# Issuing the scores of two narrow attention steps together, and moving four pieces of work, in a one-core hybrid decoder layer

## The reference, cut to what matters

```python
def dsa_attention(q_lat, kv_lat, q_idx, k_idx, w_idx, bias_tab):   # A: 8 heads
    ...
    logits = jnp.einsum('bqhc,bqkc->bqhk', ql, kv_sel) * ATTN_SCALE + bias
    ...
    p = jax.nn.softmax(logits, axis=-1).astype(kv_sel.dtype)
    return jnp.einsum('bqhk,bqkc->bqhc', p, kv_sel)

def diff_attention(q, k, v, lam, bias_tab):                        # B: 4 heads, 2 maps each
    ...
    logits = jnp.einsum('bqhmd,bshmd->bmhqs', qb, k) * ATTN_SCALE + bias
    logits = jnp.where(dist >= 0, logits.astype(jnp.float32), -jnp.inf)
    p = jax.nn.softmax(logits, axis=-1)
    attn = (p[:, 0] - lam * p[:, 1]).astype(v.dtype)
    return jnp.einsum('bhqs,bshe->bqhe', attn, v)
```

## Time and profile before

| what | value |
|---|---|
| time, median of 3 (lowest to highest) | 1002.81 us (1002.26 to 1003.08) |
| profiled execution: time, span | 1003.18 us, 1001.4 us |
| granted TensorE clock, share of full | 0.998 |
| TensorE busy | 984.4 us, 98% of the span |
| VectorE, ScalarE, GpSimd busy | 481.1 (48%), 378.6 (38%), 102.5 us (10%) |
| branch B and its drain | about 355 to 426 us of the span |

### The profile page before, as it was taken

How to read it: one execution, slowest core, us unless ns; L and a number is a source line. 1 busy time by engine, 2 the same in 40 slices (tenths; PEclk the granted TensorE clock), 3 DMA queues, 4 the chain that set the end, 5 groups by cost and what they waited for, 6 DMA issues and landing times.

```text
span 1001.4 us, 12705 instructions
## 1 busy us (share of the span) xinstructions
PE 984.4 (98%) x4925; PEld 805.3 (80%) x4925; DVE 481.1 (48%) x827; ACT 378.6 (38%) x679; POOL 102.5 (10%) x137
## 2 busy tenths in 40 slices
PE   7999999999999999999999999999999999999997
PEld 5778888878878767788788888988888888888886
DVE  4754777832244445564655563643433333331324
ACT  5345422254466666443223233542322322221222
POOL 1500000000064612200000002000000000000401
PEclk9999999999999999999999999999999999999999
DMA  8884226312131201255555642123344334222312
GB/s 329 261 267 140 85 84 174 99 43 85 63 108 32 64 23 32 74 197 174 182 183 204 221 153 84 63 84 105 108 142 153 120 105 147 84 105 84 126 43 84
DMA packets 88163, 123.13 MB, mean 123 GB/s; under 512 B 4824, under 2 KB 69941, under 8 KB 87986
## 3 DMA queue, kind: packets, MB, share of 16 engines
q1 hardware_dynamic: 87442, 115.98, 35.4%
q0 software_dynamic: 528, 6.22, 2.1%
q10 hardware_dynamic: 144, 0.26, 0.1%
HBM read 119.77 MB, written 8.45 MB: 128 GB/s over the span
## 4 chain that ended last, share of the span: by engine, by line
PE 91%; DMA 3%; DVE 2%; issue 2%; ACT 1%; POOL 1%; SPq 0%; POOLq 0%; DVEq 0%; ACTq 0%
PE tile_ps L859 18%; PE tile_ps L861 18%; PE tile_ps L860 18%; DMA w_raw<-in_w_in_dram 2%; PE t_ps L1125 2%; PE s_ps L1107 2%; PE o_ps L1154 2%; PE tile_ps L1303 1%; PE s_ps L1304 1%; PE s_ps L1303 1%; PE t_ps L1304 1%; PE t_ps L1303 1%; PE tile_ps L1302 1%; PE tile_ps L1304 1%; PE s_ps L1302 1%
## 5 line engine op out<-in xcount | busy, mean ns | idle before, releaser
L859 PE MATMUL tile_ps<-h_hi,w_hi 128*128 128x512 f32 x736 | 291.4, 396 | 1.6 <-DVE w_lo L1814 1.0
L860 PE MATMUL tile_ps<-h_lo,w_hi 128*128 128x512 f32 x736 | 286.9, 390 | 0.0
L861 PE MATMUL tile_ps<-h_hi,w_lo 128*128 128x512 f32 x736 | 286.8, 390 | 0.0
L1814 DVE TENSOR_TENSOR w_lo<-w_raw,w_hi 128x2048 fp32r<-128x2048 f32 (+3 forms) x60 | 131.3, 2189 | 162.1 <-ACT w_hi L1428 162.1
L859 PEld LDWEIGHTS tile_ps<-h_hi,w_hi 128*128 128x128 f32 x736 | 138.1, 188 | 38.9 <-issue 8.2
L861 PEld LDWEIGHTS tile_ps<-h_hi,w_lo 128*128 128x128 f32 x736 | 138.2, 188 | 29.4
L860 PEld LDWEIGHTS tile_ps<-h_lo,w_hi 128*128 128x128 f32 x736 | 138.3, 188 | 27.4 <-issue 0.2
L1428 ACT ACTIVATE w_hi<-w_raw 128x2048 fp32r<-128x2048 f32 (+3 forms) x60 | 107.3, 1788 | 42.7 <-PE tile_ps L861 9.1
L1811 DVE TENSOR_TENSOR t_lo<-t_raw,t_hi 128x2048 fp32r<-128x2048 f32 (+1 forms) x15 | 32.8, 2184 | 85.6 <-ACT t_hi L1426 85.5
L1426 ACT ACTIVATE t_hi<-t_raw 128x2048 fp32r<-128x2048 f32 (+1 forms) x15 | 27.0, 1799 | 81.5 <-PE s_ps L1304 53.5
L1573 ACT ACTIVATE nl<-nl,cst 128x256 f32<-128x256 f32 (+3 forms) x81 | 42.8, 529 | 35.8 <-DVE cst L2023 35.3
(11 more groups left out here) (404 smaller groups left out, 1680.8 us busy)
## 6 DMA issues: line engine op xcount, KB each, us to landing
w_raw<-in_w_in_dram SPq DMA_DIRECT2D x31, 1024.0 KB, 5.4
w_raw<-in_w_gate_up_dram SPq DMA_DIRECT2D x22, 1024.0 KB, 7.0
ada<-in_w_ada_dram SPq DMA_DIRECT2D x12, 1024.0 KB, 5.5
t_raw<-in_w_down_dram SPq DMA_DIRECT2D x10, 1024.0 KB, 5.0
row_copies<-row_flat POOLq DMA_DIRECT2D x1, 5632.0 KB, 21.5
ada<-in_w_ada_dram SPq DMA_DIRECT2D x8, 640.0 KB, 11.5
ada<-in_w_ada_dram SPq DMA_DIRECT2D x8, 512.0 KB, 4.3
ada<-in_w_ada_dram SPq DMA_DIRECT2D x8, 384.0 KB, 10.0
```

Source lines behind the costliest of these rows:

```text
L859: pe.matmul(dst[0:mw, :], wh, x_hi[:, kx, :], start=start, stop=False)
L860: pe.matmul(dst[0:mw, :], wh, x_lo[:, kx, :], start=False, stop=False)
L861: mm = pe.matmul(dst[0:mw, :], wl, x_hi[:, kx, :], start=False, stop=stop)
L1814: dve.tensor_tensor(w_lo[s][:, 0:kt, 0:n_cols], w_raw[s][:, 0:kt, 0:n_cols], w_hi[s][:, 0:kt, 0:n_cols].bitcast(F32), ALU.subtract) \
```

## The change

Scores in branch B: at every step with v % 4 == 0 TensorE now issues the scores of v and of v + 1 together, in the order map 0 of v, map 0 of v + 1, map 1 of v, map 1 of v + 1; those of v + 1 are written to columns 128 to 383 of the same bank. Steps with v % 4 == 1 issue no scores. VectorE's shift waits for the whole bank.

Gate tiles: Z_STEPS changes, so that steps 69, 73 and 77 have no dense piece, and 75, 79 and 83 have one. The high part of chunk 22 follows its tile; its low part stays at step 76.

GpSimd: `power(2, ...)` now stands ahead of `row_copies`, and the copies wait for the high part of chunk 4 (the third of its buffer) and no longer for h.

Branch A's reciprocals: both steps of a pair are done at the odd step.

```diff
-Z_STEPS = (66, 69, 72, 76, 80, 84)
+Z_STEPS = (66, 70, 74, 78, 81, 84)
...
+def shares_bank(v):
+
+    return v >= MIX_B and v % 4 == 1
+
+
+def paired_subs(v):
+
+    return [k for m in range(2) for k in (subs_of(v)[m], subs_of(v + 1)[m])]
+
+
+def scores_in_bank(k):
+
+    v = mix_of(k)
+    if v < MIX_B or v % 4 > 1:
+        return k + 1
+    return subs_of(v // 4 * 4)[0] + 2 * (k % 2) + 2
...
-    return {2: 15, 10: 16, 18: 17, 26: 18, MIX_A + 5: 19, MIX_A + 21: 20, Z_STEPS[0] + 2: 21, Z_STEPS[2] + 4: 22,
+    return {2: 15, 10: 16, 18: 17, 26: 18, MIX_A + 5: 19, MIX_A + 21: 20, Z_STEPS[0] + 2: 21, Z_STEPS[2] + 2: 22,
...
+            power(2, rs_kv, ms_kv, 4)
             pool.wait_ge(rows_stored, 16 * 4)
-            pool.wait_ge(h_ready, KT)
+            pool.wait_ge(w_hi_made[0], 3)
             pool.dma_start(rep_dram, row_dram.to_broadcast([P, FL_W])).then_inc(rows_copied, 16)
-            power(2, rs_kv, ms_kv, 4)
...
-                if k >= 2:
+                if k >= 2 and not shares_bank(v):
                     pe.wait_ge(shifted, k - 1)
...
-                    mm = pe.matmul(ps[:, 0:w], bqk[DH * m:DH * m + DH, h, i * P:(i + 1) * P],
+                    c0 = P if shares_bank(v) else 0
+                    mm = pe.matmul(ps[:, c0:c0 + w], bqk[DH * m:DH * m + DH, h, i * P:(i + 1) * P],
...
-                for u in steps_begun_at(v):
-                    for k in subs_of(u):
+                if v >= MIX_B and v % 4 == 0 and v < N_MIX:
+                    for k in paired_subs(v):
                         scores(k)
+                elif v < MIX_B or v % 4 > 1:
+                    for u in steps_begun_at(v):
+                        for k in subs_of(u):
+                            scores(k)
...
-                dve.wait_ge(scores_made, k + 1)
+                dve.wait_ge(scores_made, scores_in_bank(k))
...
-                if v % 2 == 0 and v < MIX_B:
-                    reciprocal(v - 1)
                 for u in steps_begun_at(v):
                     shift(subs_of(u)[0])
-                if v % 2 or v == MIX_B:
-                    reciprocal(v - 1)
+                if v % 2:
+                    for u in (v - 1, v):
+                        reciprocal(u)
```

More of the change, by code:

```diff
@@ L2022, in shift @@
                     dve.wait_ge(transposed, before + 1)
-                dve.tensor_tensor_reduce(out=b[:, 0:w], in0=s_ps[k % 2][:, 0:w], in1=table, scale=1.0, scalar=3e38,
+                c0 = P if shares_bank(v) else 0
+                dve.tensor_tensor_reduce(out=b[:, 0:w], in0=s_ps[k % 2][:, c0:c0 + w], in1=table, scale=1.0, scalar=3e38,
                                          op0=ALU.add, op1=ALU.min, accum_out=negmax[:, k:k + 1]) \
```

## The result

The changed kernel takes 1007.67 us (median of 6 runs, 1006.71 to 1009.21) against 1003.09 us (6 runs, 1002.26 to 1003.95) for the kernel before: a ratio of 1.0043, 95% interval 1.0033 to 1.0053. It is slower by 3.3 to 5.3 us. The forecast was 1003.1, no change, with 1005.2 as the upper end of its range.

A forecast was written before the change was run, and what follows sets the result against it. TensorE, busy 984.4 of 1001.4 us, was taken to bound the kernel. Gains of 1.0, 0.9, 1.65 and 1.0 against waits of 4.8 gave +0.25: 1003.1 us on the median's basis, range 1000.8 to 1005.2.

The forecast's parts named there:

- Part 1: GpSimd's bias-row copies moved behind chunk 4 and the power: TensorE's wait for chunk 4's low half goes, -1.0 us.
- the two bounds: Chunk 8's load under the later copies: landing at 126.2, costing nothing (taken), or ready at 134.0, 1.0 us late.
- Part 2: Branch A, reciprocals of a pair together: the wait at the transposes of step 51 goes, -0.9 us.
- Part 3: Branch B, scores of two narrow steps merged into a group of 0.84 us: -1.65, and -1.0 at step 76.
- step 76: Branch B: its scores no longer wait for the shifts of 75, since 75 now has a piece, -1.0 us.
- 0.41 a head, -1.65 for four: Merged scores in branch B: 0.42 + 0.63 becomes 0.84 and one dear first matmul falls away in each head.
- one dear first matmul: First projection matmul behind scores takes 0.42 us where the next takes 0.23; merging was to save one a head.
- Part 4: Branch B, steps 69, 73 and 77 without scores or projection, and the sixth gate tile: new TensorE waits, together +4.8 us.
- 0.75, 1.75, 1.5 and 0.8: New waits in us: transposes of 67, scores of 70, output transposes of head 1, sixth gate tile.
- The first rival: VectorE reaches mix and shift before TensorE, so the new branch B waits shrink: down to 998.3 us, chance 0.14.
- the second: Rival: the later copies starve chunk 8's load, +1.0 us (1004.1) or +2.2 (1005.3), chance 0.13.
- the third: Rival: the merged group's maps follow one another, 1.26 us instead of 0.84, giving 1003.9, chance 0.08.

The follow-up runs named there:

- recip_alone: The kernel before with only the new order of branch A's reciprocals: 0.9998 of before.
- the mended pair: Changed kernel with low halves of chunks 21 and 22 later and two bv tiles evicted earlier: 0.9979 with merged scores, 0.9983 with each step's scores separate.
- pairs_alone: The kernel before with only the merged scores, gate pieces where they were: branch B's stretch 74.78 us against 74.79.
- zsteps_alone: The kernel before with only the moved gate pieces, chunk 22's low half kept at step 76: 1006.29 us, 1.0040 of before.
- the two make_lo moves: Changed kernel with chunk 22's low half made at step 78, not 76: 1004.17 us; with chunk 21's also at 70, not 68: 1002.87 us.
- lo22_later: Changed kernel with VectorE's low half of chunk 22 made at step 78 in place of 76: 1004.17 us.
- before_stall: The kernel before, with VectorE making chunk 22's low half once and a half more for nothing: 1008.55 us, 1.0058 of before.

## Why the prediction was wrong

**Part 1 was right**, in mechanism and size (-1.0 forecast, 1.27 in the trace, 0.9985 alone). Chunk 8 landed between the two bounds and was hidden.

**Part 2 failed.** The step is "Issued with the even step's, it is ready 3 us sooner: -0.9"; it brought nothing (7.47 against 7.54 in the trace). The normalisation is sooner, but I didn't follow what stands next: the up-projection waits 1.1 for the eviction of bv, late for the same reason. recip_alone shows it, and the edit that evicts early frees 1.25 there in the trace.

**Part 3 failed in its worth, not in the price of the group.** The merged group costs 0.86 as summed, and step 76 gained its 1.0. The step that failed is "0.41 a head, -1.65 for four", in two ways. About half of the 0.41 is the "one dear first matmul" that falls away. But Part 4 leaves steps 69, 73 and 77 without a projection, so there is none left there to start cheaply: the moved pieces pay the dear start elsewhere, as at 75 behind the scores (395.61, 0.43 in the chain above), and head 0 had no gate piece in step 65. What is left is the 0.2 a head of the mended pair. And it took TensorE's saved time for the kernel's: in pairs_alone, where the pieces stay, head 2 gains 0.35, and the others lose theirs to ScalarE and VectorE, so the stretch kept its length to 0.01.

**Part 4 was right in place and near in size.** Forecast 0.75, 1.75, 1.5 and 0.8; the waits are 0.7, 1.2 (and 0.4 more for the second map's start: the scores then take 1.25 by their records where 0.85 is usual), 1.9 and 0.7. zsteps_alone and the two make_lo moves show the mechanisms: the low halves in front of the shift and in front of the scaling.

**What no step had** is the half clock behind the wait at head 1: 1.8 us, by lo22_later. Branch B's 5.47 then adds up from runs: the moved pieces alone 3.30 (zsteps_alone; Part 4 with step 76 was summed at 3.8), the half clock 1.8, and the merging on top of the moved pieces +0.4 (80.26 - 1.8 - 78.09, with the longer wait at head 1 in it) where -1.65 was forecast. With part 1's 1.27 that is +4.2, and the ratio says +4.3. The first rival is wrong (the waits were not covered), the second is wrong (chunk 8 was in time), the third too.

Left open: whether the half clock comes in each execution. The mean granted clock of the whole execution is 0.996 in three of the changed kernel's six runs (1007.4 to 1009.2 us) and 0.998 in the other three (1006.7 to 1008.0), as it is in the kernel before; in before_stall it is 0.996 in two of five. In no listed run of the other kernels is it under 0.997. 3.4 us at half the clock take 0.002 off the mean, so it probably came in those five runs alone, but the runs without a trace don't show it. The forecast fails without it too: the three runs at 0.998 are all above 1005.2.

## What to carry to other kernels

Where one engine is busy for 98%, time saved on it counts only up to the next wait: follow each gain on to what the engine reaches next, and ask what that one is waiting for. A step without work of its own on the busy engine is a window on the latency of the others, so before a filler is moved, look for the long instruction of another engine (here a 2.3 us make_lo) that it was covering, and move that first. A wait may cost more than its length when the clock falls behind it. And when a change has several parts, take the saving of one from the kernel that the others leave: here one part counted a start that another had moved elsewhere.

## What the hardware showed that was not expected

A wait of 1.86 us, in an engine otherwise busy nearly all the time, was followed by 3.4 us at the 1.2 GHz level (405.4 to 408.8, by the shares in the stretches), and one of 2.9 us by 6.8 us (407.8 to 414.6); two waits of 1.2 us each in zsteps_alone were followed by none. By the mean clocks, waits like the first two were not followed by it in every execution. A load of 1024 KB that usually lands in 5.4 us took 24.8 us under the 5632 KB of copies; these were issued at 102.1 and took 21.3, so it landed 5 us after them. Two matmuls on the upper half of the rows, behind two on the lower half in the program, ran beside them: 128 + 256 columns on each half in 0.86 us.
